# A decoder trunk on one core: the weight combinations of its block products are made by GpSimd instead of VectorE

## The reference

```python
def swiglu(x, w_gate, w_up, w_down):
    return (jax.nn.silu(x @ w_gate) * (x @ w_up)) @ w_down
...
    x = x + 0.5 * swiglu(rmsnorm(x, ffn1_norm), ffn1_w_gate, ffn1_w_up, ffn1_w_down)
...
    x = x + 0.5 * swiglu(rmsnorm(x, ffn2_norm), ffn2_w_gate, ffn2_w_up, ffn2_w_down)
```

## Time and profile before

| | |
|---|---|
| median of 3 runs | 2095.47 us (2095.33 to 2097.08) |
| the profiled execution | 2097.14 us, span 2095.4 us |
| mean granted TensorE clock | 0.998 |
| first FFN's block products (groups 0 to 27) | 565.33 us from 57.77 |
| second FFN's block products | 565.15 us from 1451.41 |
| share of the chain that ended last | PE 92%, of which line 997 (block products) 54% and line 867 (other projections) 28%; DVE 3%, ACT 2% |

### The profile page before, as it was taken

How to read it: one execution, slowest core, us unless ns; L and a number is a source line. 1 busy time by engine, 2 the same in 40 slices (tenths; PEclk the granted TensorE clock), 3 DMA queues, 4 the chain that set the end, 5 groups by cost and what they waited for, 6 DMA issues and landing times.

```text
span 2095.4 us, 37492 instructions
## 1 busy us (share of the span) xinstructions
PE 2084.1 (99%) x15762; PEld 2053.8 (98%) x15762; DVE 1469.6 (70%) x1361; ACT 866.0 (41%) x1288; POOL 946.4 (45%) x580
## 2 busy tenths in 40 slices
PE   9999999999999999999999999999999999999998
PEld 9999999999999999999999999999999999999998
DVE  7878667676654568878788596786766766675546
ACT  7433333352322235678786540124333333352324
POOL 4644445456643322352534552324554445464650
PEclk9999999999999999999999999999999999999999
DMA  5133232363523322310112422131222232456132
GB/s 174 62 122 122 82 121 103 142 223 122 182 86 111 107 81 101 123 54 32 54 43 71 153 81 95 43 129 61 102 101 102 110 114 83 177 187 227 57 122 81
DMA packets 83383, 227.48 MB, mean 109 GB/s; under 512 B 9608, under 2 KB 18312, under 8 KB 83216
## 3 DMA queue, kind: packets, MB, share of 16 engines
q1 hardware_dynamic: 82064, 224.56, 30.2%
q10 hardware_dynamic: 1152, 0.52, 0.1%
HBM read 162.05 MB, written 63.17 MB: 107 GB/s over the span
## 4 chain that ended last, share of the span: by engine, by line
PE 92%; DVE 3%; ACT 2%; DVEq 1%; issue 1%; DMA 0%; ACTq 0%; POOL 0%; SPq 0%; POOLq 0%
PE banks L997 54%; PE banks L867 28%; PE banks L911 3%; PE banks L1267 2%; PE banks L1178 0%; ACT gate_a L1543 0%; PE banks L1025 0%; PE banks L1032 0%; PE banks L1038 0%; PE banks L1156 0%; PE banks L1174 0%; ACT gate_x L1543 0%; PE banks L1148 0%; DVE decay L2212 0%; DVEq L2177 0%
## 5 line engine op out<-in xcount | busy, mean ns | idle before, releaser
L867 PE MATMUL banks<-u_hi,w_lo 128*128 128x344 f32 x864 | 286.1, 331 | 0.6 <-DVE lru_even L1748 0.3
L867 PE MATMUL banks<-u_hi,w_hi 128*128 128x344 f32 x864 | 276.2, 320 | 0.0
L867 PE MATMUL banks<-u_lo,w_hi 128*128 128x344 f32 x864 | 275.8, 319 | 0.0
L740 POOL TENSOR_TENSOR w_lo<-w_raw,w_hi 128x1024 fp32r<-128x1024 f32 (+1 forms) x68 | 167.1, 2458 | 166.3 <-DVE xbc L2183 123.6
L738 POOL TENSOR_SCALAR w_hi<-w_raw 128x1024 fp32r<-128x1024 f32 (+1 forms) x59 | 67.0, 1135 | 344.1 <-PE banks L867 276.5
L867 PEld LDWEIGHTS banks<-u_hi,w_lo 128*128 128x128 f32 x864 | 162.7, 188 | 7.5 <-issue 4.9
L867 PEld LDWEIGHTS banks<-u_hi,w_hi 128*128 128x128 f32 x864 | 162.7, 188 | 5.1 <-issue 4.3
L867 PEld LDWEIGHTS banks<-u_lo,w_hi 128*128 128x128 f32 x864 | 162.8, 188 | 0.0
L997 PE MATMUL banks<-mix_hi,w_lo 128*128 128x258 f32 x864 | 158.1, 282 | 0.0
L997 PE MATMUL banks<-mix_hi,w_hi 128*128 128x258 f32 x864 | 157.9, 282 | 0.0
L997 PE MATMUL banks<-mix_hi,w 128*128 128x258 f32 x832 | 151.6, 283 | 0.0
(11 more groups left out here) (374 smaller groups left out, 6671.1 us busy)
## 6 DMA issues: line engine op xcount, KB each, us to landing
w_raw<-in_gate_up SPq DMA_DIRECT2D x46, 512.0 KB, 4.2
hidden<-up SPq DMA_DIRECT2D x44, 516.0 KB, 3.6
raw<-in_gate_up SPq DMA_DIRECT2D x40, 512.0 KB, 4.0
w_raw<-in_w_in SPq DMA_DIRECT2D x36, 512.0 KB, 4.0
hidden_mix<-hidden_part SPq DMA_DIRECT2D x16, 1032.0 KB, 4.7
slot_raw<-hidden_mix SPq DMA_DIRECT2D x16, 1032.0 KB, 6.0
slot_raw<-hidden SPq DMA_DIRECT2D x12, 1032.0 KB, 6.5
raw<-in_down SPq DMA_DIRECT2D x16, 512.0 KB, 4.4
```

Source lines behind the costliest of these rows:

```text
L740: pool.tensor_tensor(w_lo[s][:, 0:n], w_raw[s][:, 0:n], w_hi[s][:, 0:n].bitcast(F32), ALU.subtract).then_inc(split, 1)
L867: end = pe.matmul(out[:, c, 0:CH], w[s][:, k * P:(k + 1) * P], x[kx][:, c * CH:(c + 1) * CH], start=(first and n == 0), stop=(last and n = ...
```

## The change

From the third group on (q > 1), GpSimd makes the weight combinations of a group itself, in its own queue between the low part of p2's operand and that of p6's. VectorE makes only those of groups 0 and 1. The combinations are five operations instead of four, since a21 + a22 is made first, used for s0, and then negated by an operation of its own. What they wait for is as before: both weight tiles, and the low part of p3's operand of the group before. The other engines' queues are as they were.

```diff
+            def weight_sums(f, q):
+
+                first, second = f.raw[2 * q % 4], f.raw[2 * q % 4 + 1]
+                a11, a12, a21, a22 = first[:, 0:512], first[:, 512:1024], second[:, 0:512], second[:, 512:1024]
+                for n in range(2):
+                    pool.wait_ge(*f.raw_landed[(2 * q + n) % 4].past(16 * (q // 2 + 1)))
+                pool.wait_ge(*f.op_ready.past(7 * q - 1))
+                pool.drain()
+                pool.tensor_tensor(f.s[1][:], a11, a21, ALU.subtract)
+                pool.drain()
+                pool.tensor_tensor(a21, a21, a22, ALU.add)
+                pool.drain()
+                pool.tensor_tensor(f.s[0][:], a21, a11, ALU.subtract)
+                pool.drain()
+                pool.tensor_scalar(a21, a21, -1.0, 0.0, ALU.mult, ALU.add)
+                pool.tensor_tensor(f.s[2][:], a12, f.s[0][:], ALU.subtract).then_inc(f.sums_ready.sem, 1)
+
...
                 for q in range(NGT):
                     for name in ORDER:
+                        if name == "p6" and q > 1:
+                            weight_sums(f, q)
                         operand(f, q, name)
...
                     return {"p2": lambda: product(f, q // 2, 0), "p6": lambda: product(f, q // 2, 1),
-                            "p5": lambda: weight_sums(f, q + 1), "p7": more}
+                            "p7": more}
 
                 def odd(q):
-                    return {"p6": lambda: weight_sums(f, q + 1), "p5": extra.get(q)}
+                    return {"p5": extra.get(q)}
...
                     if q == NG - 1:
-                        between = {"p2": lambda: slot_low(f, 0), "p5": lambda: (weight_sums(f, NG), slot_low(f, 1)),
+                        between = {"p2": lambda: slot_low(f, 0), "p5": lambda: slot_low(f, 1),
                                    "p7": lambda: slot_low(f, 2), "p3": lambda: slot_low(f, 3)}
...
                 for q in range(NG, NGT):
-                    between = dict(hooks.get(q, {}))
-                    if q < NGT - 1:
-                        between["p7"] = lambda q=q: weight_sums(f, q + 1)
-                    down_group(f, q, between)
+                    down_group(f, q, hooks.get(q, {}))
```

## The result

| | before | after |
|---|---|---|
| median | 2096.27 us (2095.33 to 2097.19, 4 runs) | 2118.73 us (2117.26 to 2119.40, 4 runs) |
| ratio, 95% interval | | 1.0104 (1.0092 to 1.0117) |
| span of the profiled execution | 2095.4 us | 2116.8 us |
| block products of the first FFN | 565.33 us | 633.62 - 57.58 = 576.04 us |
| block products of the second FFN | 565.15 us | 2037.95 - 1462.36 = 575.59 us |

The change costs 22.5 us, five times what a measurement of this kernel can tell from no change. The two product stretches are longer by 10.71 and 10.44 us, 21.15 together; the span grew by 21.4. So the loss lies in the two FFNs, nearly all of it. (In experiments 4, 10 and 12 one execution each was disturbed and much longer, 6677.6, 2242.55 and 3409.03 us; the times given there are medians of the other executions, and the trace of experiment 4, which is of the disturbed one, is not read.)

The account below looks back on a forecast made before the run. TensorE bounds the kernel, waiting for nobody in the FFNs' block products. Seams at groups 20 and 24 cost 7.8 + 3.3 = 11.1 us per FFN, 22.2 in all: 2095.47 + 22.2 = 2117.7, say 2118; range 2108 to 2138.

Parts of the forecast that it names:

- a set, undisturbed: One group's weight combinations on GpSimd, five operations, take 6.2 us; back to back without gaps 5.5.
- p6 of group 21 late: After group 20's delay, GpSimd hands over p6's low part of group 21 at 495.2, due at 494.3: 1.0 us more.
- per FFN: Loss at both seams of one FFN: 7.8 + 3.3 = 11.1 us; the second FFN the same.
- Gate/up hidden: Gate/up groups: GpSimd's set fits before p6's operand is due, so these groups cost nothing.
- 4 us of cover: Gate/up groups: p6's operand is ready 6 us early, less 2.2 us of pushes by VectorE's mixes.
- 15 of 20.2: Gate/up groups: GpSimd's work per group, 7 × 1.25 + 6.2 = 15 of 20.2 us.
- GpSimd becomes the bound in every group: Rival: one microsecond in each of 18 gate/up groups of both FFNs, 36 us more, 2154; chance 0.10.
- The seam at group 20: Cover is two products shorter: p6 starts 4.6 us late, group 20 ends 6.8 late; with group 21, 7.8 us.
- The seam at group 24: Second block's slots are split here: p6 of group 24 1.8 us late, of group 25 1.5, together 3.3 per FFN.
- The clock added nothing: Low clock after TensorE's stalls is mostly absorbed by later waits: 0 added, upper bound 12 us.
- the rival: In the clock point: the low clock costs its full price, 2 us for each of three stalls per FFN, 2130; chance 0.10.
- No gain by a closer pitch: Against the rival that matmuls run closer than 2.884 us per product, giving no loss or a gain; chance 0.10.

Follow-up runs that it names:

- experiment 4: Kernel before the change, but GpSimd makes the sets of groups 24 and 25 alone: 2102.48 us against 2096.15, ratio 1.0028.
- experiment 10: Changed kernel with one GpSimd operation more in the sets of groups 2 to 19: 2118.97 us against 2118.73.
- experiment 12: Changed kernel with 34 extra matmuls in TensorE's queue before p6 of group 20, in both FFNs: 2117.35 us.
- experiment 1: Changed kernel, but VectorE makes the sets of groups 20, 21, 24 and 25 again: 2097.31 us against 2095.58 for the kernel before, ratio 1.0004.
- experiment 2: Kernel before the change, but GpSimd makes the sets of groups 20, 21, 24 and 25 only: 2119.18 us against 2095.58, ratio 1.0109.
- experiment 8: Changed kernel with two GpSimd operations more in the sets of groups 2 to 19: 2160.80 us.
- experiment 3: Kernel before the change, but GpSimd makes the set of group 20 alone: 2110.52 us, ratio 1.0067.
- experiment 11: Changed kernel, but ScalarE makes slot 4's high part before p6's high part of group 20, not behind it: 2119.68 us.
- experiment 7: Changed kernel with one GpSimd operation more in the sets of groups 20, 21, 24 and 25: 2132.14 us.
- experiment 6: Changed kernel with the sets of groups 20, 24 and 25 earlier in GpSimd's queue: 2103.31 us against 2096.79 for the kernel before, ratio 1.0031.

## Why the prediction was right

The time (2118 forecast, 2118.73 measured) is right by its steps, which can be held against the trace one by one. That it is right to 0.7 us is partly luck: the product stretches grew by 21.15 instead of 22.2, and the medians by 22.46, in which the spread between executions has its part.

| step of the prediction | forecast | measured |
|---|---|---|
| a set, undisturbed | 6.2 us | 291.46 to 297.68: 6.22; its negation 0.63 |
| set 20 ends | 469.6 | 469.69 |
| p6 of group 20 starts | 471.85 | 471.91 |
| ScalarE reaches the slot's high part | 470.25 | 470.32 |
| p5's and p7's low parts end | 475.7, 479.2 | 475.71, 479.10 |
| group 21 starts | 488.5 | 488.50 |
| p6 of group 21 late | 1.0 | 495.04 - 488.50 - 5.77 = 0.77 |
| p6 of group 24 late | 1.8 | 557.28 - 495.04 - 21 x 2.884 = 1.68 |
| p6 of group 25 late | 1.5 | 578.58 - 557.28 - 20.19 = 1.11 |
| per FFN | 11.1 | 10.7 and 10.4 |
| VectorE's and GpSimd's busy time | -144 or more, +300 | -209.7, +334.6 |

- **Gate/up hidden: right, with less room than I gave.** They run without a break but for some 0.3 us in the first FFN (group 20 starts 404.03 us after its first product, before 403.71), and experiments 1 and 2 show that 44 sets cost nothing. The 4 us of cover was wrong as a measure. It is how late one set may be; a set that is longer in every group is covered only by GpSimd's spare time per group, 2.35 us by the waits of experiment 10. I had that number in reach ("15 of 20.2") and made it too large, 5.2, because the hand-over of 0.8 and the longer operations beside VectorE were not in it. The rival "GpSimd becomes the bound in every group" fell, but a set some 3 us longer would have made it true (experiment 8), and through a waiter that I didn't name: ScalarE's copy of p1.
- **The seam at group 20: right to 0.1 us, but in the first FFN not by the waits that were forecast behind p6.** Those of p5, p7 and p3 (1.1, 0.6 and 0.5 us) are not in the trace: p6 ran at half speed and took their 2.2 us. With the clock kept up (experiment 12) they are there: p5 starts 1.13 us later than the pitch of 2.88 behind p6, p7 0.52 and p3 0.44. Set 20 alone costs 7.0 and 6.7 us (experiment 3). That ScalarE's order makes p5, p7 and p3 late is only one form of it: with the other order the wait falls on p6 (6.23 us), with the low clock on top (experiment 11).
- **The seam at group 24: right, somewhat large** (2.8 against 3.3), and it stands by itself (experiment 4). In the second FFN the same 1.68 us comes in two parts: TensorE restarts at p4 of group 23 after a late join (1952.08) and again at p6 of 24 (1961.64).
- **The clock added nothing: right here, for the reason given** (experiment 12). After group 24's stall of 1.54 us the granted clock was 1.00 throughout, so there was nothing to pay. But the rival was no idle one: in experiment 7 a wait of 2.80 us was followed by 0.50 with the next operand ready, and cost another 2.4 us. That stall was paid twice, as would follow from the rule of the Trainium skill that the prediction quotes (TensorE: Matmul & The Clock Gate, Part 1: The HAM clock gate).
- **No gain by a closer pitch: right.** 2.884 us per product, with VectorE's 60% as with its 70%.

## What to carry to other kernels

Where the bounding engine runs without a pause, work moved off another engine gains nothing, and its price is decided where the receiving engine's queue is tightest, not on the average: here 8 of 52 sets made the whole loss, and the average load (61%) said nothing about them. Work out two covers for a moved step, how late one may be and how much spare time the receiver has per period with hand-overs and slowed neighbours counted; the smaller one holds. And look past the operand itself to what stands behind it in the engines between, since the wait may surface at an instruction that has nothing to do with the moved work.

## What the hardware showed that I had not expected

- One more two-input operation of 512 columns per group took about 2 us of GpSimd's time in gate/up instead of 1.44. I take it that it and its neighbours met VectorE's two-input work more often: VectorE's busy time in the same stretch grew too, from 137.9 to 143.1 us for the same 139 instructions.
- A one-input operation is held by a slot split like a two-input one: the negation of 0.62 us took 2.48 at 452.70 in experiment 6.
- After the 4.38 us wait the granted clock was still 0.50 in 474 to 476 and 0.83 in 476 to 478, though the products had resumed at 471.91 and TensorE was busy throughout. After the 1.54 us wait at group 24 it never left 1.00.
